# One block for all stages, an fp32r slot table, and TensorE joining the two experts' rows in the last stage

## The reference

```
x1  = layer_norm(ALPHA*x + (1+g1)*(y_mixer @ w_out))
hm  = x1*(1+sc2) + sh2
probs = softmax(hm @ w_router + b_router)          # 32 experts in 4 groups
group = argmax(sum of the two best of each group)  # then the two best inside it
gates = their two probabilities, normed to sum 1
y   = sum over the two experts of gate * (silu(hm@w_gate)*(hm@w_up)) @ w_down
out = layer_norm(ALPHA*x1 + (1+g2)*y)
```

## Time and profile before

| | |
|---|---|
| time, median of 3 | 2988.47 us |
| the profiled execution: its time, its span | 2990.43 us, 2988.6 us |
| mean granted TensorE clock | 0.958 of 2.4 GHz |
| busy: TensorE, VectorE | 2718.9 us (91%), 2218.1 us (74%) |
| busy: ScalarE, GpSimd | 1315.9 us (44%), 1489.7 us (50%) |
| bytes moved | 610 MB |
| output projection | about 1542 to 1964 us |
| experts, table and loop | 1975 to 2866 us |
| last stage | 2873 to 2988 us |

### The profile page before, as it was taken

One profiled execution on the slowest core, in us unless ns is written; L12 is line 12 of the kernel. 1 busy time (PEld: TensorE's weight loads), 2 busy tenths in 40 slices (PEclk: granted clock), 3 DMA queues, 4 the chain that ended last, 5 costly groups with the idle time before them and its releaser, 6 DMA issues. The chain is left out here.

```text
span 2988.6 us, 41030 instructions
## 1 busy us (share of the span) xinstructions
PE 2718.9 (91%) x14603; PEld 2316.1 (77%) x14603; DVE 2218.1 (74%) x2647; ACT 1315.9 (44%) x1655; POOL 1489.7 (50%) x755
## 2 busy tenths in 40 slices
PE   3899999999999999999979999949999999999920
PEld 2688888888889888888868888747888888888820
DVE  7678777777878777887863333458888888888857
ACT  4443333343433333343431111126777777777733
POOL 0133433343343334334432222126899999999963
PEclk9899999999999999999989999959999999999965
DMA  8844544444553544455252322249878869678676
GB/s 271 310 183 145 211 155 171 174 171 161 184 211 137 190 175 165 166 184 197 95 169 106 105 105 105 78 152 373 319 269 293 307 242 341 233 259 288 245 273 247
DMA packets 253185, 610.13 MB, mean 204 GB/s; under 512 B 15968, under 2 KB 98560, under 8 KB 244864
## 3 DMA queue, kind: packets, MB, share of 16 engines
q1 hardware_dynamic: 228208, 525.26, 49.2%
q0 software_dynamic: 11520, 41.95, 3.7%
q10 hardware_dynamic: 13328, 41.21, 3.4%
HBM read 600.75 MB, written 99.89 MB: 234 GB/s over the span
## 5 line engine op out<-in xcount | busy, mean ns | idle before, releaser
L1933 DVE TENSOR_TENSOR piece_lo<-piece_raw,piece_hi 128x2048 fp32r<-128x2048 f32 x187 | 563.3, 3031 | 102.5 <-ACT piece_hi L2040 101.3
L2040 ACT CAST piece_hi<-piece_raw 128x2048 fp32r<-128x2048 f32 x280 | 526.7, 1910 | 217.8 <-issue 77.8
L1933 POOL TENSOR_TENSOR piece_lo<-piece_raw,piece_hi 128x2048 fp32r<-128x2048 f32 x93 | 558.9, 6010 | 34.5 <-ACT piece_hi L2040 32.3
L574 PE MATMUL op<-hm,w_hi 128*128 128x512 f32 x2048 | 533.4, 406 | 45.2 <-DVE hm L1236 45.2
L1110 DVE SCALAR_TENSOR_TENSOR cv<-ub,par,cv 128x512 f32<-128x512 f32 x384 | 381.0, 992 | 157.1 <-ACT cv L833 147.9
L574 PEld LDWEIGHTS op<-hm,w_hi 128*128 128x128 f32 x2048 | 379.8, 190 | 119.5 <-DVE hm L1236 45.2
L524 POOL TENSOR_TENSOR xw<-xw,t 128x512 f32<-128x512 f32 x64 | 98.7, 1543 | 488.6 <-DVE t L1178 488.5
L589 PE MATMUL pz<-wz_hi,hm 128*128 128x256 f32 x2048 | 296.9, 290 | 1.1 <-DVE wz_lo L1088 0.5
L589 PEld LDWEIGHTS pz<-wz_hi,hm 128*128 128x128 f32 x2048 | 266.8, 192 | 7.4 <-DVE wz_lo L1088 3.9
L574 PE MATMUL op<-hm,w_lo 128*128 128x512 f32 x1024 | 254.9, 391 | 0.0
L505 POOL TENSOR_TENSOR xdt<-xw,tab 128x512 f32<-128x512 f32 x64 | 70.4, 1100 | 369.3 <-ACT xw L852 345.1
(11 more groups left out here) (338 smaller groups left out, 5698.2 us busy)
## 6 DMA issues: line engine op xcount, KB each, us to landing
hm<-hm_parts SPq DMA_DIRECT2D x30, 4096.0 KB, 13.9
piece_raw<-in_w_gate SPq DMA_DIRECT2D x94, 1024.0 KB
piece_raw<-in_w_up SPq DMA_DIRECT2D x94, 1024.0 KB
piece_raw<-in_w_down SPq DMA_DIRECT2D x92, 1024.0 KB
decay<-acum_rows SPq DMA_DIRECT2D x32, 1024.0 KB
w_raw<-in_w_in SPq DMA_DIRECT2D x48, 512.0 KB, 7.5
expert_out<-ye ACTq DMA_DIRECT2D x46, 512.0 KB
w_ada_part<-in_w_ada_t SPq DMA_DIRECT2D x32, 512.0 KB, 3.9
```

The costliest lines, as they stand in the source:

```text
L574: mm = nc.tensor.matmul(pj[m % 2][:], wp[m][:, kk, :], hm[b][:, hp, kk, :], start=q == 0, stop=q == 3 * KK - 1)
L1933: v.tensor_tensor(lo[q][:], raw[q][:], hi[q][:].bitcast(F32), ALU.subtract).then_inc(lo_done[q], 1)
L2040: nc.scalar.copy(hi[q][:], raw[q][:]).then_inc(hi_done[q], 1)
```

## The change

All stages now stand in one block, with no block end between them. The semaphores of a finished part are cleared along the way, by GpSimd in the projection's second step and by SP between its stores of the last stage. Buffers get places in SBUF by hand (spacers named `unused`).

At the start of the projection SP asks for the five broadcast rows before the scan's last store; tile 1's second half of products goes ahead of tile 0's transposes; and tile 2's y is loaded, cast and lowered before `mix_rows`:

```diff
+            sp.wait_ge(o.rows_out, 16)
+            sp.wait_ge(gt, 2 * STEPS)
+            sp.dma_start(k.g1[:], k.adad[0].partition_broadcast(P)).then_inc(out_sems.row_in, 16)
+            for row, source, piece_low in ((k.b2, k.adad[1], 12), (k.a1, k.d["ln_g"][0], 13),
+                                           (k.b1, k.d["ln_b"][0], 14), (k.a2, k.adad[2], 15)):
+                wait_low(sp, o, piece_low)
+                sp.dma_start(row[:], source.partition_broadcast(P)).then_inc(out_sems.row_in, 16)
             store(LAST, 1)
...
-            final = isinstance(i, int) and i == TT - 1
-            if before and not final:
+            behind = isinstance(i, int) and i in (1, TT - 1)
+            if before and not behind:
                 turn(i - 1)
             if here:
                 products(b, 1)
-            if final:
+            if isinstance(i, int) and i == EARLY + 2:
+                logits(EARLY)
+            if behind:
                 turn(i - 1)
-            if before:
+            if before and not (isinstance(i, int) and i == EARLY + 1):
                 logits(i - 1)
...
         def step(i, b):
 
+            if in_loop(i, 1) and not in_loop(i, 2):
+                low(i + 1, 1 - b)
+                mix_rows()
             if in_loop(i, 1):
                 tile(i - 1, 1 - b)
-            if in_loop(i, 1, TT - 1):
+            if isinstance(i, int) and i == TT - 1:
+                choose(0, 0, EARLY)
+            if in_loop(i, 2, TT - 1):
                 low(i + 1, 1 - b)
-            if not in_loop(i, 1):
-                mix_rows()
-            if isinstance(i, int) and i == TT - 2:
-                choose(0, 0, EARLY)
```

As the last hunk shows, the first round of the routing stands behind tile 14. ScalarE's exp for it stands in the step of tile 14, behind the wait for logits(13). In the same step function ScalarE makes the first expert's high parts, and VectorE low parts around `choose(1)`; SP asks for these weights as soon as the last products are done:

```diff
+                if isinstance(j, int) and j == TT - 1:
+                    first_high(0)
+                    first_high(1)
                 if in_loop(j, 1, TT):
                     act.wait_ge(lg_mm, j)
+                if isinstance(j, int) and j == TT - 2:
+                    power(0, EARLY)
...
+        sp.wait_ge(o_mm, 2 * TT)
+        for q in range(x.PIECES):
+            sp.dma_start(x.raw[q][:], first_weights(k, q)).then_inc(x.loaded[q], 16)
...
         loop(dve, step, 1)
+        first_low(0)
+        first_low(1)
         choose(1, EARLY, TT - EARLY)
+        first_low(2)
         dve.wait_ge(pos_mm, 2)
```

In the last stage gathers run four tiles ahead instead of eight and there are four output tiles instead of two. ScalarE makes two diagonal matrices of the gates, TensorE sums both experts' rows into PSUM, in fp32, and VectorE's sum reads them there:

```diff
+            for gate, diag in ((k.gate_a, dga), (k.gate_b, dgb)):
+                nc.scalar.activation(diag[i % 2][:], k.ident[:], ACT.Copy, scale=gate[:, i:i + 1]).then_inc(dg_done, 1)
...
+            pe.wait_ge(dg_done, 2 * (i + 1))
+            if i >= 2:
+                pe.wait_ge(r_done, i - 1)
+            for diag, y, arrived, n in ((dga, ya, ya_in, 0), (dgb, yb, yb_in, 1)):
+                pe.wait_ge(arrived[s], 16 * (i // R + 1))
+                for h in range(2):
+                    mm = nc.tensor.matmul(both[b][:, h * 512:(h + 1) * 512], diag[b][:],
+                                          y[s][:, h * 512:(h + 1) * 512], start=n == 0, stop=n == 1,
+                                          skip_group_check=True)
+            mm.then_inc(ms_done, 1)
...
-                nc.vector.tensor_tensor_reduce(out=r[b][:], in0=ya[s][:], in1=xa[s][:], scale=1.0, scalar=0.0,
+            nc.vector.tensor_tensor_reduce(out=r[b][:], in0=both[b][:], in1=xa[s][:], scale=1.0, scalar=0.0,
                                                op0=ALU.add, op1=ALU.add, accum_out=total[b][:]).then_inc(r_done, 1)
```

More of the change, by code:

```diff
@@ L198, in mixer_steps, with first_weights @@
+def first_weights(k, q):
+    if q < 4:
+        return k.d["w_gate" if q < 2 else "w_up"][0].rearrange("(kk p) f -> p kk f", p=P)[:, (q % 2) * 4:(q % 2) * 4 + 4, :]
+    return k.d["w_down"][0].rearrange("(kk p) f -> p kk f", p=P)[:, :, (q - 4) * 512:(q - 3) * 512]
+def mixer_steps(nc, k, first, out):
     with ExitStack() as ctx:
-        own = ExitStack()
+        own, later, own_sems = ExitStack(), ExitStack(), ExitStack()
+        stay = k.semaphores
         sb, ps, sem = k.makers(own)
@@ L260, in mixer_steps @@
         k.later()
-        o = projection_buffers(k, ctx, first)
+        o = projection_buffers(k, later, first)
+        later.close()
+        k.semaphores, kept = own_sems, len(k.used)
         k.g1, k.a1, k.b1, k.a2, k.b2 = o.g1, o.a1, o.b1, o.a2, o.b2
@@ L309, in mixer_steps @@
                  "t1_done y_done yn_done sq_done xdt_done xend_done xd_done y3 gt ms_done rs_done").split())
+        of_mixer = k.used[kept:]
+        k.semaphores = stay
+        out_sems = projection_semaphores(k)
+        own_sems.close()
+        of_projection = [s for s in k.used if s not in of_mixer]
+        k.used = of_projection
+        of_experts = ExitStack()
+        x = experts_buffers(k, of_experts)
+        of_experts.close()
+        k.used = []
+        w = output_buffers(k, ctx)
+        w.used = k.used
+        k.used = of_projection
         block = ctx.enter_context(nc.Block())
@@ L1556, in step @@
             nc.gpsimd.tensor_tensor(r[:], r[:], k.b1[:], ALU.add).then_inc(xa_done, 1)
+            if not in_loop(i, 2) and in_loop(i, 1):
+                for s in of_mixer:
+                    pool.sem_clear(s)
         loop(pool, step)
@@ L1659, in step @@
             j = i - 1
+            if in_loop(i, 1) and not in_loop(i, 2):
+                split(i + 1, 1 - b)
             if in_loop(j, 0, TT):
@@ L1689, in _ @@
         loop(act, step, 1)
[L1690 to L1691 removed]
+        first_high(4)
+        first_high(5)
     @block.vector
@@ new lines, in _, with low_part @@
+        sp.wait_ge(arrived.xa_out, 16 * TT)
+        sp.dma_start(w.xa[0][:], k.xad[0]).then_inc(w.xa_in[0], 16)
+        last = loop(sp, step)
+        for n in range(1, OUT_RING):
+            if n % 2:
+                sp.wait_ge(lo_done[(n - 1) // 2], 2 * last + 3)
+                sp.sem_inc(k.passed, 1)
+            sp.dma_start(w.xa[n][:], k.xad[n]).then_inc(w.xa_in[n], 16)
+    def low_part(eng, v, q, t):
+        if in_loop(t, 1):
+            eng.wait_ge(used[q], t)
+        eng.wait_ge(hi_done[q], t + 1)
+        v.tensor_tensor(lo[q][:], raw[q][:], hi[q][:].bitcast(F32), ALU.subtract).then_inc(lo_done[q], 1)
@@ L2418, in program @@
             first = [ps(f"op0{n}", [P, 512]) for n in range(2)]
-            stage(nc, k, mixer_steps, first)
-            if stop > 2:
-                stage(nc, k, experts, first)
-        if stop > 4:
-            stage(nc, k, output, out)
+            stage(nc, k, mixer_steps, first, out)
     return k
```

969 lines of the change are left out of this document (512 added, 457 removed).

## The result

The changed kernel takes 2967.4 us (median of 4 runs, 2965.5 to 2969.4) against 2988.3 (4 runs), a ratio of 0.9923 with a 95% interval of 0.9912 to 0.9935: 21 us faster. 2950 was forecast, with a range of 2936 to 2970: the sign holds and the time lies in the range, but 17 us above the forecast and outside the forecast's own range of 2942 to 2957. The profiled run took 2968.0, its span is 2966.2, 22.4 less than before.

| stretch | before | after | difference | forecast |
|---|---|---|---|---|
| up to the projection's own first products | 1542.4 | 1541.0 | -1.4 (drift) | |
| from there to turn(2) | 75.7 | 81.1 | +5.4 | -2 |
| turn(2) to the table's first instruction | 356.9 | 355.4 | -1.5 | -2 |
| the table, to the ids | 23.6 | 21.6 | -2.1 | -2 |
| ids to the first expert product | 9.5 | 11.7 | +2.2 | 0 |

A forecast was written before the change was run, and what follows sets the result against it. TensorE, busy 91%, was taken to bound the kernel, so gains lay at stage joints and in the VectorE-bound last stage. Terms of -40.5 from 2990.4 gave 2950, 2948 at the median's level; +2 made 2950, range 2936 to 2970.

The forecast's parts named there:

- those at the routing's end: Signs: VectorE waits about 14 us for choose(0)'s exp; the table's first instruction comes 2 to 3 us after choose(1).
- Last stage: First gather to last norm: VectorE loses a step, TensorE joins; 82 us instead of 109.5, so -27.5.
- transfers pace the last stage: Rival, last stage: tiles still take 6.1 us, the stage 109, total 2977; chance 0.12.
- Joins at 1.2 GHz: Rival, TensorE in the last stage: joins stay at half clock, 7.4 us a tile, total 2998; chance 0.06.
- Boundary: Last expert store to first gather: GpSimd waits for the store itself, first gather about 2869.0; -4 us.
- table: Table of slots: single-pass fp32r products remove VectorE's 2.01 us wait; -2 us.
- end of the projection: Routing's end: choose(0) follows tile 14, block boundary goes, table begins at 1973.0 instead of 1975.05; -2 us.
- the routing's end costs more: Rival: rank products all at 1.2 GHz, casts in the way of turn(15); +8 us, total 2958; chance 0.15.
- Start of the projection: Rows asked for earlier, tile 2's y halves lowered before mixing; logits(0) as good as 1580.2 instead of 1582.0; -2 us.
- no hole: Rival: TensorE has no hole at the projection's start; -12 us, total 2938; chance 0.08.
- First expert tile: First to second expert tile: no GpSimd low parts, tile 1's pieces asked for at once; -3 us from 20.4.
- Tail: End of the kernel: SP's semaphore clearing between loads and stores shows at the end; +2 us.

The follow-up runs named there:

- e6: Changed kernel with the last stage's joins given back to ScalarE's scaling pass and one VectorE step: 2975.5 us, 8.1 more.
- e7: Changed kernel with the eight x loads within the last stage left out: 2957.7 us (2 runs), 9.7 less; stage 75.2 us.
- e11: Kernel before, with its own blocks and loads, given only TensorE's joins by diagonals in its last stage: 2976.3 us, ratio 0.9960.
- e3: Changed kernel with the exp of choose(0) put ahead of ScalarE's wait for logits(13): 2956.9 us, 10.5 less.
- e4: Changed kernel with the two norm rows and first x loaded behind the experts' loop instead of ahead of its first weights: 2962.7 us, 4.7 less.
- e1: Changed kernel with the rows mixed before tile 2's first y half is lowered, and the second half behind tile 0: 2958.5 us, 8.9 less.
- e2: Changed kernel with only the mixing moved ahead of tile 2's two low halves, both still before tile 0: 2960.5 us, 6.9 less.
- e5: Changed kernel with VectorE's last low part of tile 0's weights put behind x's two low halves: 2962.6 us (2 runs).
- e10: Changed kernel with e1, e3, e4, e5, twelve x tiles ahead, gathers seven ahead, SP's clearing done two tiles earlier: 2933.9 us.
- four mends: The edits of e1, e3, e4 and e5 made together in the changed kernel: 2940.6 us, 26.8 less.
- e12: As e10, but the gathers' lead grows step by step from four tiles to eight: 2936.0 us; stage 81.5 us.

## Why the prediction was right and where it failed

The sign and the range held. Of the signs that the prediction named, those at the routing's end came, and in the last stage TensorE's clock of 1.00, with a period of 3.8 to 5.0 us (once 6.2) where 4.2 to 5.1 was named. The others did not come. It wanted a hole of about 5 us at the projection's start (11.50), the second expert tile 9 us earlier (4.9 later) and the first gather 13 earlier (0.9 later). A table that begins after 1975 was to show it wrong, and it began at 1977.48. The time is in the range since the last stage, most of the sum, came out near its term, and that in part by luck.

*Last stage, -27.5, measured -25.6.* The number is close by luck: two terms were off and cancel. VectorE's period is 3.80, not the 4.25 taken from the row of before: the pow is 0.56 us instead of 1.53 and VectorE no longer waits for it. e6 shows the cause as far as runs here go: with the sum's operands back in SBUF the pow takes 1.54 again, starting 0.12 us behind that sum. This is the rule that the prediction weighed (the Trainium skill, GPSIMD Engine Reference, Specifications), and the trace agrees with it; the 77 us that it gave for the stage did not come, because transfers then set the pace. Their term, +3.5, was too small: tiles 5 to 13 lose 10.9 us in all against a period of 3.80, and e7 puts the x loads alone at 8.7. The smaller period gives back 7.2 (16 x 0.45), so the two nearly cancel. The rival "transfers pace the last stage" was right on the mechanism in these nine tiles and wrong on the price (5.0 us a tile, not 6.1). Alone, the joins bring 13.0 us (e11) and the rest of the change in this stage 14.1 (e6), together 25.6: the two parts hardly overlap.

*Joins at 1.2 GHz.* Refuted: 1.00 in the stretch above. Only the first join begins at half clock (3.75 us for the first two of its four products, 2.48 for the others); it ends 10.5 us behind the first gather, 9.2 costed.

*Boundary, table, end of the projection.* -3.6, -2.1 and -1.5 against -4, -2 and -2, each by the mechanism named: the store's landing alone (3.4 us from its issue at 2870.59 to the first gather, 2.6 put), ids that wait for nothing, a chain that `choose(0)`'s exp holds 13.4 us. That wait had been costed and not questioned: e3 shows that it is one line's place in ScalarE's queue and that 9.3 us come back without it. The rival "the routing's end costs more" did not come.

*Start of the projection, forecast -2, measured +5.4: the step that failed.* The two halves of y took what was costed: 13.5 us from the request to the end of the second low part, 13.2 forecast (its own 7.2 a half would have given 14.4). What was wrong is when they begin. SP was said to be free at 1541.7 as before, but its first request goes at 1545.96, 4 us late, since it waits for the last two stores of the scan (L474). These land 6.7 and 7.7 us after their issue, and 1.9 and 2.0 in the kernel before. The five rows, 2.6 MB, are now asked for just ahead of them and still under way; no run put the store first again, so that cause is read from the traces and not tested. With it, mixing begins 19.9 us behind the projection's first products instead of 15.6: 4.3 of the 7.4 us between forecast and measurement.

Most of the rest, about 2.5 us, is a wait that was not costed. The clock lost behind the hole was counted (2 us); but then products(3) wait for tile 3's low half (0.80 us) and run in part at half clock behind it. That second loss of clock is not in every profile: it stands in five of the seven that start like this, behind waits of 0.80 to 2.09 us, and not in e4 (1.64 us) and e6 (0.38).

The order on VectorE, mixing behind both halves, had been costed and not questioned. The pair of e1 and e2 says what it is worth: with the mixing first the stretch is 3 us shorter than before the change (72.8), with the second half behind tile 0 6.5 shorter (69.3). That is still less than the 14 of the rival "no hole" (-12 on top of -2), since waits and half clock come back in smaller pieces.

*First expert tile, forecast -3, measured +2.3, with +2.2 ahead of it.* Here the delay by the three loads was too small. Their bytes were priced (3.9 us), and the third piece of tile 1 was put at 17 us behind the gathered rows of tile 0; it is cast 19.7 us behind them (15.2 before). The loads stand before the pieces in both SP's queue and the transfers': the pieces are asked for 3.7 us after TensorE has the gathered rows (2007.39), 2.2 in e4, and the first is cast 10.6 us after its request, 6.7 in e4. With the loads out of the way the tile takes 17.9 us, 2.5 less than before, near the -3. That GpSimd's low parts had gone was taken as a gain; that VectorE's own low part would lie beside GpSimd's copy of the ids was not seen. e4 and e5 return 6.2 and 2.3 (2.0 up to the second tile).

*Tail.* +2.3 against +2, but for another reason than SP's clearing, as e10 shows. The last store is issued at 2957.93 and lands 2.6 us later, so 5.7 of the 8.3 us lie behind all work that the trace shows. What makes them is open; e11 clears the joins of it, and no run tried the number of blocks or the four output tiles.

The terms summed to -38.5 with the tail, the profile says -22.4. Of the 16.1 us between, the start holds 7.4, the first expert tile with the copy ahead of it 7.5, the last stage 1.9; drift takes 1.4 back and the rest is 0.7.

## What to carry to other kernels

When an edit frees an engine of a wait, read what stands next in that engine's own queue: all four mends here are the order of a few lines in an engine's own queue, and they gave 26.8 us together, more than the change itself. Work moved ahead of a stage is moved in front of something, on the issuing queue as well as in bytes: here rows in front of a store, and norm rows in front of weights. And where two parts of a change meet in one stage, one part alone in the old kernel and one part undone in the new one tell their shares in two runs.

## What the runs showed of the hardware

Here GpSimd's small instructions, beside a VectorE instruction that reads two operands of SBUF, end with it or take as long as it does: the copy of 128 ids ends at 2001.87, VectorE's low part beside it at 2001.82, and it is 0.19 us alone (e5); the pow is 0.56 beside a sum with one operand in PSUM and 1.54 beside a sum of two in SBUF (after and e6). It goes the other way too: of two low parts on VectorE after the change, 2.29 us each by themselves, the one that begins at 1959.28 takes 4.46, beside GpSimd's add of 2.36 us from 1959.23. The Trainium skill (SBUF — State Buffer, SBUF: two separate sides) calls it an exclusive lock, held for the whole instruction by whichever started first. The traces agree with a wait to the end. With who wins they agree at 1959, where GpSimd's record starts 0.05 us ahead and VectorE waits, and not at 1999, where GpSimd's starts 0.13 us ahead (1999.42) and GpSimd waits; so the start of a record does not tell.

A single-pass product of 128 x 66 in fp32r takes half the records of the fp32 one: sixteen in 3.60 us here, at half clock, against 32 records for sixteen products in 7.03. A gather costs GpSimd 1.25 us from issue to issue, so fourteen of them hold it for 17.1 us (e10, 2844.80 to 2861.95); that, and not only the transfers, limits how far ahead it pays to gather (e10, e12).
